# Attention of a four-layer encoder in pairs of heads: row-tiled scores, value matmuls of 512 columns, raw copies of q and k, an output projection with banks of its own

## The reference, cut to what matters

```python
for i in range(DEPTH):                      # DEPTH = 4, mixer i % 3
    h = rms_norm(x, attn_norm[i])
    proj = h @ w_in                         # 1024 x 3072 (FoX, REL) or 1024 x 1280 (SWA)
    q, k = rms_norm per head (16 heads of 64; SWA has 2 k/v heads, and rope)
    s = q @ k.T / 8 (+ cumulated log gates | + rel bias | window), masked
    o = softmax(s) @ v                      # SWA: one sink logit more in the softmax
    x = x + o @ w_o[i]
    x = x + conv_ffn(rms_norm(x, ffn_norm[i]), ...)
    x = x + sigmoid(rms_norm(x, ple_norm[i]) @ w_ple_gate[i]) * (p[i] @ w_ple_proj[i])
```

## Time and profile before

| | us |
|---|---|
| median of 3 runs (1481.05 to 1485.66) | 1484.01 |
| the profiled execution | 1480.81 |
| its span, first to last instruction | 1479.0 |
| PE busy | 1407.5 (95%) |
| DVE busy | 987.0 (67%) |
| ACT busy | 808.8 (55%) |
| POOL busy | 381.8 (26%) |

### The profile page before, as it was taken

The page is one execution under the profiler, slowest core; times in us unless marked ns, Lnnn a source line. Parts: engine busy times, 40 slices in busy tenths (PEclk is TensorE's granted clock), DMA queues, the critical chain, the costliest instruction groups (busy, mean ns, idle before and its releaser), DMA issues. The chain is left out here.

```text
span 1479.0 us, 24840 instructions
## 1 busy us (share of the span) xinstructions
PE 1407.5 (95%) x8532; PEld 1235.1 (84%) x8532; DVE 987.0 (67%) x1577; ACT 808.8 (55%) x1397; POOL 381.8 (26%) x437
## 2 busy tenths in 40 slices
PE   5999899999999999999987989999999999999998
PEld 4877799988777779998876779998878777999986
DVE  4657677764666867775476867776466575777644
ACT  4546566653555756664354656665356464666533
POOL 2311033320144603331027103332014110233200
PEclk9999999999999999999998899999999899999999
DMA  8522365564564345556552136666455322665651
GB/s 284 169 88 86 102 201 184 182 200 151 183 199 129 114 152 177 184 183 199 163 185 87 58 103 198 186 181 198 152 183 169 116 86 73 198 185 184 196 174 57
DMA packets 63959, 233.00 MB, mean 158 GB/s; under 512 B 7216, under 2 KB 7344, under 8 KB 63888
## 3 DMA queue, kind: packets, MB, share of 16 engines
q1 hardware_dynamic: 61056, 221.87, 46.7%
q0 software_dynamic: 2832, 10.18, 2.2%
HBM read 230.97 MB, written 1.05 MB: 157 GB/s over the span
## 5 line engine op out<-in xcount | busy, mean ns | idle before, releaser
L616 DVE TENSOR_TENSOR w_lo<-w_raw,w_hi 128x1024 fp32r<-128x1024 f32 x418 | 544.5, 1342 | 125.6 <-ACT w_hi L386 124.6
L386 ACT ACTIVATE w_hi<-w_raw 128x1024 fp32r<-128x1024 f32 x418 | 419.6, 1052 | 151.1 <-PE bank L1087 113.1
L1063 PE MATMUL bank<-hT_hi,w_hi 128*128 128x256 f32 x1408 | 398.7, 283 | 4.3 <-DVE hT_lo L670 4.3
L1064 PE MATMUL bank<-hT_lo,w_hi 128*128 128x256 f32 x1408 | 398.5, 283 | 0.0
L1065 PE MATMUL bank<-hT_hi,w_lo 128*128 128x256 f32 x1408 | 398.4, 283 | 0.0
L1063 PEld LDWEIGHTS bank<-hT_hi,w_hi 128*128 128x128 f32 x1408 | 270.3, 192 | 5.1 <-issue 5.1
L1064 PEld LDWEIGHTS bank<-hT_lo,w_hi 128*128 128x128 f32 x1408 | 270.3, 192 | 0.0
L1065 PEld LDWEIGHTS bank<-hT_hi,w_lo 128*128 128x128 f32 x1408 | 270.3, 192 | 0.0
L1049 POOL TENSOR_TENSOR gate_c<-gate_c,up_c 128x256 f32<-128x256 f32 x88 | 105.1, 1194 | 289.0 <-ACT gate_c L591 289.0
L901 DVE SCALAR_TENSOR_TENSOR gate_c<-bank,conv_sb,gate_c 128x255 f32<-128x255 f32 (+1 forms) x176 | 84.1, 478 | 116.2 <-ACT up_c L587 116.2
L1063 PE MATMUL bank<-w_hi,hT_hi 128*128 128x512 f32 (+1 forms) x336 | 137.3, 409 | 12.4 <-DVE w_lo L616 6.6
(11 more groups left out here) (141 smaller groups left out, 2237.1 us busy)
## 6 DMA issues: line engine op xcount, KB each, us to landing
w_raw<-weights SPq DMA_DIRECT2D x418, 512.0 KB, 4.0
gain<-gains POOLq DMA_DIRECT2D x11, 512.0 KB, 4.6
rel<-rel_in POOLq DMA_DIRECT2D x4, 512.0 KB, 6.5
x<-x_in SPq DMA_DIRECT2D x2, 512.0 KB, 6.5
p_raw<-p_in POOLq DMA_DIRECT2D x4, 256.0 KB, 5.0
out<-x SPq DMA_DIRECT2D x2, 512.0 KB, 2.6
gain<-gains SPq DMA_DIRECT2D x1, 512.0 KB, 7.0
consts<-consts_in POOLq DMA_DIRECT2D x1, 488.0 KB, 5.8
```

Of the source, the lines that this page charges most:

```text
L386: nc.scalar.activation(w_hi[:, slot, q * HALF:(q + 1) * HALF], w_raw[:, raw, :], ACT.Copy).then_inc(hi_ready, 1)
L616: nc.vector.tensor_tensor(w_lo[:, slot, cols], w_raw[:, half(q)[0], :], w_hi[:, slot, cols].bitcast(F32), ALU.subtract).then_inc(lo_ready, 1)
L1063: nc.tensor.matmul(out_ap, l_hi, r_hi, start=start, stop=False, skip_group_check=True)
L1064: nc.tensor.matmul(out_ap, l_hi, r_lo, start=False, stop=False, skip_group_check=True)
```

## The change

- **Order of the blocks**: q0, k0, q1, k1, v0, v1; the weights are laid out to match. The first eight pieces after the opening pair (blocks q1 and k1) come before the attention; the eight pieces of v0 and v1 come in steps 0 to 5 of it (2, 2, 1, 1, 1, 1).
- **Items**: ACT copies q or k raw into `qn` (now three deep) and squares it; PE may overwrite the bank after these two. POOL scales the item in `qn` (FoX, REL). In SWA DVE scales it and makes one rope product, POOL the other product and the sums.
- **Attention**: eight steps of a head pair. Scores alternate between the two row groups (rows 0 to 63 and 64 to 127) into two banks, and the first query tile sees only 128 keys. `sel` and `cum` are doubled to 64 rows in each group. All probabilities are scaled by POOL, none by DVE. The values of a pair are 3 matmuls of 512 columns (both heads) and 3 of 2x128 columns.
- **Banks**: transposed items in `aux[2..3]`; the output projection in `acc[0]`, `acc[1]`, `aux[0]`, `aux[1]`, so both token tiles of a unit can run together; embedding's projection in `aux[2..3]` and `acc[2..3]`, placed around the transposes of the norm.
- **Rest**: one `gain` buffer instead of two, the relative bias in pairs of heads and not negated, no zero blocks in `pT`.

```diff
+STEP_PIECES = {FOX: {0: (8, 9), 1: (10, 11), 2: (12,), 3: (13,), 4: (14,), 5: (15,)}, SWA: {}}
+ITEMS_AFTER_PIECE = {FOX: {1: (2,), 3: (3,), 6: (4,), 7: (5,)}, SWA: {0: (2,), 3: (3,)}}
+STEP_ITEMS = {FOX: {1: (6, 7)}, REL: {1: (6, 7)}, SWA: {1: (4,), 2: (5,)}}
+STEP_O = {FOX: {6: 0, 7: 1}, REL: {6: 0, 7: 1}, SWA: {5: 0, 7: 1}}
+STEP_V = {FOX: {2: (0, 1), 5: (2,), 6: (3,)}, SWA: {}}
+STEP_SPLITS = {FOX: {1: (16,), 2: (17, 18), 3: (19,), 4: (20,), 5: (21,), 6: (22,), 7: (23,)},
+               SWA: {0: (8,), 1: (9,)}}
 ...
 # ACT
+                for s in range(PAIRS + 3):
+                    if s >= 3:
+                        round_o(s - 3)
+                    if s < PAIRS:
+                        exps(2 * s)
+                        exps(2 * s + 1)
+                        if m == SWA:
+                            sink_exps(s)
+                    for i in STEP_ITEMS[m].get(s - 1, ()):
+                        copy_items(i)
+                    for j in STEP_V[m].get(s + 0, ()):
+                        evacuate_v(j)
+                    if 1 <= s <= PAIRS:
+                        round_pT(2 * s - 2)
+                        round_pT(2 * s - 1)
+                    for j in STEP_SPLITS[m].get(s, ()):
+                        split_half(first, j)
 ...
 # DVE
+                for s in range(PAIRS + 3):
+                    if s < PAIRS:
+                        mask_scores(2 * s)
+                        mask_scores(2 * s + 1)
+                        if m == SWA:
+                            sink_sums(s)
+                    if s >= 3:
+                        rest_o(s - 3)
+                    if m == SWA and s < 2:
+                        turn_item(4 + s)
+                    for i in STEP_ITEMS[m].get(s - 1, ()):
+                        rest_items(i)
+                    for j in STEP_V[m].get(s, ()):
+                        rest_v(j)
+                    if s < PAIRS:
+                        invert_sums(s)
+                    if 1 <= s <= PAIRS:
+                        rest_pT(2 * s - 2)
+                        rest_pT(2 * s - 1)
+                    for j in STEP_SPLITS[m].get(s, ()):
+                        split_half(first, j)
 ...
 # POOL: the items first, then the pairs
+                def normalise_p(h):
+                    for c, qb in ((slice(0, P), 0), (slice(P, 3 * P), 1)):
+                        nc.gpsimd.tensor_scalar(sc[:, h % SC, c], sc[:, h % SC, c], den[:, qb, h:h + 1], 1.0,
+                                                ALU.mult, ALU.mult).then_inc(pn_ready, 1)
+                for s in range(PAIRS):
+                    if m == REL and s + 2 < PAIRS:
+                        pool.wait_ge(s_min, 2 * (HEADS * L + 2 * s + 2))
+                        load_bias(s + 2)
+                    if m == REL and s and s + 1 < PAIRS:
+                        prepare_bias(s + 1)
+                    pool.wait_ge(rden_ready, PAIRS * L + s + 1)
+                    normalise_p(2 * s)
+                    normalise_p(2 * s + 1)
 ...
 # PE
+                def piece(j):
+                    i, g, t = todo[j]
 ...
+                        elif i == 4:
+                            pe.wait_ge(sq_ready, item0 + 4 + t + 1)
+                        else:
+                            pe.wait_ge(v_ready, FIRST_V[L] + t + 1)
 ...
+                def score_pair(pair):
 ...
+                    for qb in range(2):
+                        keys = P if qb == 0 else SEQ
 ...
+                        for left, right in ((qT_hi, kT_hi), (qT_hi, kT_lo), (qT_lo, kT_hi)):
+                            for e, r in enumerate(halves):
+                                last = nc.tensor.matmul(aux[e][:, cols], left[r, pair, ts], right[r, kp, 0:keys], ...
 ...
+                for s in range(PAIRS + 2):
+                    if s < PAIRS:
+                        score_pair(s)
+                    for j in STEP_PIECES[m].get(s, ()):
+                        piece(j)
+                    if s in STEP_O[m]:
+                        o_piece(STEP_O[m][s], 0)
+                    if s == PAIRS:
+                        o_piece(0, 1)
+                    if 1 <= s <= PAIRS:
+                        transpose_p(2 * s - 2)
+                        transpose_p(2 * s - 1)
+                    transpose_items(*STEP_ITEMS[m].get(s, ()))
+                    if s >= 2:
+                        values(s - 2)
+                    if s == PAIRS:
+                        o_piece(1, 1)
+                o_piece(2, 0)
+                o_piece(2, 1)
+                o_piece(3, 0).then_inc(tile_done, 1)
+                o_piece(3, 1)
```

More of the change, by code:

```diff
@@ L153, in trunk @@
         hT_lo = sb("hT_lo", [P, KC, SEQ], F32R)
-        gain = sb("gain", [P, 2, D])
+        gain = sb("gain", [P, D])
         ident = sb("ident", [P, P])
@@ L383, in split_hi @@
                     act.wait_ge(raw_landed[raw], loads * 16)
-                    if not first and q == 0:
+                    if not first and q == halves[0]:
                         act.wait_ge(unit_used, u - (RING - 1))
@@ L498, in evacuate @@
                         ins.then_inc(v_hi_ready, 1)
-                if L == 0:
[L501 to L525, removed]
@@ new lines, in _ @@
+                if m == SWA:
+                    item_rstd(0)
+                    turn_item(0)
+                    item_rstd(1)
+                    item_rstd(2)
+                    turn_item(1)
+                    turn_item(2)
+                    for i in range(3, len(ITEMS[m])):
+                        item_rstd(i)
+                        turn_item(i)
+                else:
+                    for i in range(len(ITEMS[m])):
+                        if i == 6 and m == REL:
+                            prepare_bias(0)
+                            prepare_bias(1)
+                        item_rstd(i)
+                        scale_item(i)
@@ L1230, in transpose_p @@
+                        if m == FOX:
+                            for e, r in enumerate(halves):
+                                h = 2 * pair + e
+                                last = nc.tensor.matmul(aux[e][:, cols], sel[r, h:h + 1].to_broadcast([HD, P]), cum[r, 0:keys],
+                                                        start=False, stop=True, skip_group_check=True)
+                                if qb == 1:
+                                    last.then_inc(s_done, 1)
                 def transpose_p(h):
@@ L1282, in _ @@
[L1282 to L1284 removed]
+                    if k == 0 and t == 0:
+                        if m == SWA:
+                            pe.wait_ge(sq_ready, item0 + 6)
+                        else:
+                            pe.wait_ge(v_ready, FIRST_V[L] + 4)
+                    if k == 0 and t == 1:
+                        pe.wait_ge(s_min, 2 * HEADS * (L + 1))
@@ L1342, in in_units @@
         out.append(w[:, :, -256:].transpose(1, 0, 2).reshape(P, UNIT))
-    for c in range(0, w.shape[2] - 511, 512):
+    for c in order or range(0, w.shape[2] - 511, 512):
         for g in range(2):
```

741 lines of the change are left out of this document (387 added, 354 removed).

## The result

The kernel after takes 1449.79 us, median of four runs (1449.07 to 1451.53), against 1484.05 for the kernel before (1481.05 to 1485.66): ratio 0.977, interval 0.9755 to 0.9791. It is faster, by 34 us. The prediction had 1420, so its sign and its range held, and 30 of the forecast 64 us did not come. The profiled execution went from a span of 1479.0 to 1447.0.

A forecast was written before the change was run, and what follows sets the result against it. PE's work and waits in the mixers were taken as the bound. Savings 2 x 17.8 + 8.3 + 3 x 3.1 + 6.5 + 3.6 = 63.3 us from 1480.8 gave 1417.5, 1420 for the runs; range 1397 to 1458.

The forecast's parts named there:

- Scores: PE's scores of a head pair: 1.1 us in FoX, 0.86 in REL or SWA, for 3.26 and 1.8 before.
- Rival 1: Scores: row groups don't overlap when each matmul brings its own weights; + 19 us, 1439; chance 8%.
- Values and transposes: PE work of a head pair: values 1.05 us for 2 x 0.72 before, transposes staying at 0.84.
- Pace of a step: Steps holding a pair and one piece: 5.75 us in FoX, taken as 5.7, and 5.5 in REL; PE sets it.
- Rival 2: Attention steps: DVE, ACT and POOL set the round, 6.5 us, as contention stretches them; + 23 us, 1443; chance 24%.
- The wait before piece 12: FoX and REL, step 2: PE waits 5.5 us for v0's copy before v1 overwrites its bank; slower clock 3 us.
- Rival 3: Step 2 of FoX and REL: the wait for v0 is short, as DVE is ahead; - 8 x 3, 1396; chance 11%.
- two output pieces to cover the last POOL work: End of FoX mixer: steps 8 and 9 with two output pieces, 8.5 us, within a mixer of 77.5.
- REL: REL mixer, first score to end of output projection: 75.6 us for 83.9, saved 8.3.
- Before the scores: FoX and REL: PE's waits for k items go and two items' transposes move behind; 3.1 us in each of three layers.
- Late next: nothing: FoX and REL, before the scores: no new wait follows; PE runs from piece 7 into step 0.
- SWA: SWA layer: 84 us for 90.5, saved 6.5, bounds -4 and 13; PE idle 11 us before first transposes of probabilities.

The follow-up runs named there:

- e3_rows_apart: Kernel after, with a pair's scores issued head by head, all of one row group and then the other: 1452.51 us, ratio 0.9801 to the kernel before.
- e5_dve_256: Kernel after, with scaling of the 256-column block of probabilities moved from POOL to DVE: 1452.49 us, ratio 0.9781 to the kernel before.
- e6_one_op: Kernel after, with POOL's scaling as one multiplication, without the second one by 1.0: 1453.26 us, ratio 0.9793 to the kernel before.
- e2_v_early: Kernel after, with block v0 copied out in step 1 (not 2) and v1 in steps 4 and 5 (not 5 and 6): 1412.26 us, ratio 0.9521.
- e1_v1_early: Kernel after, with block v1 alone copied out one step earlier, in steps 4 and 5 in place of 5 and 6: 1431.56 us, ratio 0.9642.
- e8_item5: e2_v_early, with item 5 of FoX and REL transposed in step 0 behind the first scores, not in front of them: 1408.09 us, ratio 0.9475.
- e4_swa_pool: Kernel after, with POOL in SWA scaling pairs 0 and 1 before it turns items 4 and 5: 1448.59 us, ratio 0.9756 to the kernel before.
- e7: e2_v_early, e8_item5 and e4_swa_pool together, against the kernel before: 1399.17 us, ratio 0.9431.

## Why the prediction was right or wrong

The mechanism held: PE set the pace of the FoX and REL steps, its work for a pair fell, and most of the gain came from the two FoX layers. One term was mis-sized, by an omitted wait.

*Scores.* Forecast 1.1 and 0.86, measured 1.10 and 0.88. Rival 1 is out: the row groups overlap, in e3_rows_apart even without the alternating order. The single place in the earlier trace rows was a fair witness.

*Values and transposes.* Forecast 1.05 and 0.84, measured 1.22 and 0.58, together 1.80 for 1.89: two errors that nearly cancel. Six transposes in one run cost less each than three (0.097 for 0.14), and the three 512-column matmuls behind them took 0.78 for 3 x 0.23. Both look like a price of each change of kind; that reading was not tested.

*Pace of a step.* Forecast 5.7 to 5.75 and 5.5, measured 5.78 and 5.57. Rival 2 is out for the kernel after, and in e5_dve_256 DVE has 0.87 us more in each step, and the step stays. But here the forecast had luck. It put POOL's scaling at 3.0 a pair, from the one-operand rows, and it takes 1.8, since the kernel writes it with two operands. In e6_one_op it takes 3.3, near the forecast's own price, and there rival 2's mechanism does reach PE, in one step of each FoX and REL mixer (6.7 us), 3 us in all and not its 23. By the rule of the Trainium skill that the prediction cited, SBUF — State Buffer, section Who interferes with whom, a DVE operation with two inputs in SBUF and a POOL operation that reads SBUF contend for a pair of ports under an exclusive lock. The trace agrees about the lock: a DVE addition of 4 columns takes 1.22 us beside POOL's 1.77 us product in SWA, where both end at 799.6, and 0.15 later. The same shows on the other side at 1182.8 in layer 3, where POOL's scaling of 128 columns takes 1.42 us beside a split, for 0.37 just ahead of it. It doesn't follow that each step loses by it; in the kernel after PE's step is 5.78 all the same:

```profile
797.84 1.77 POOL L1135 TENSOR_TENSOR rope_c<-qn,rtab 128x512 f32<-128x512 f32 x1 [0.81 <-DVE qn L814]
...
798.41 1.22 DVE L957 TENSOR_TENSOR den<-den,esink 128x4 f32<-128x4 f32 x1
...
810.03 0.15 DVE L957 TENSOR_TENSOR den<-den,esink 128x4 f32<-128x4 f32 x1
```

*The wait before piece 12.* Forecast 5.5 us and a lower clock behind it for 3 us; measured 5.6 and 5.8, then a piece of 4.6 to 5.1 us for 2.9, so 1.7 to 2.2 for the clock. Rival 3 is out as a forecast. As an experiment it came true: e2_v_early gained 19.3 over e1_v1_early; I had put its advantage at 24.

*The step that failed: the FoX and REL mixers' sum, in "two output pieces to cover the last POOL work".* I gave the output pieces of steps 6 to 9 no wait. But they use the banks of v as piece 12 does: the same semaphore, `v_ready`, at a count of 4 where piece 12 asks for 1. I had worked out who copies v0 and in which step, and had not asked the same of v1. In the kernel after it costs 5.9, 6.6 and 5.9 us of waiting and 1.6 to 2.0 at the lower clock behind each, 7.9 x 3 = 24 by these lengths. Taking it out gave 18.2 us in the median, and mixers of 77.5 and 75.8 us for the forecast 77.5 and 75.6. So in its mixers the kernel that I had predicted was e1_v1_early. That they agree to 0.2 us is partly luck: in layer 3 piece 12 cost 0.7 us less than charged there (5.6 + 2.2 for 8.5), and the step with the copy 0.6 more.

*REL*: forecast 8.3 saved, measured 0 (83.9 before and after); the missed wait (6.6 + 2.0) is all of it.

*Before the scores*: forecast 3.1 each, measured 1.8 in layer 0, 2.2 in REL and 0.8 in layer 3. "Late next: nothing" was wrong:

```profile
1129.33 0.66 PE L1276 MATMUL bank<-ident,qn 128*128 128x128 f32 x4 [0.33 <-POOL qn L1125]
...
1134.25 0.66 PE L1276 MATMUL bank<-ident,qn 128*128 128x128 f32 x4 [1.49 <-POOL qn L1125]
```

PE no longer waits for the k items, but for POOL's scaling of items 4 and 5, whose transposes stand in front of the scores. I had checked POOL's chain against item 7 only. e8_item5 took the wait out.

*SWA*: forecast 6.5 saved, measured 1.3 (89.2 for 90.5). PE's idle time was called at 11 us and was 10.6, but pair 0 was scaled from + 34.5 on, not at + 29.3: POOL's turns of items 3 to 5 took 3.4 to 4.5 us each and waited up to 4.5 for DVE's product. e4_swa_pool makes the layer 5.9 shorter.

*After the mixer*: forecast 0.9 a layer, measured 0.9 (10.3 to 9.3).

The bill, forecast less saved by layer: 6.8, 9.4, 6.9 and 8.1, together 31. The missed wait is 24 of them by its lengths, and 18 by the time or 21 by the mixers of e1_v1_early. SWA's start is 5, the waits before the scores another 4 to 5, and the way from layer 1's up projection to SWA's first items 2. The mixer of layer 0 had been 1.3 us shorter than layer 3's already before, which the forecast counted as gain. Against these stand about 2.5 for the shorter stretch behind piece 12, and the 2.7 by which layer 0 started sooner. It is the missed wait that made 1420 into 1450.

What stays open: why the granted clock falls behind a short wait in one kernel and not behind the same wait in another. In e4_swa_pool it took back 4 us of 5.9, and so it blurs what an edit of that size is worth. The length of the wait alone does not decide it. Before the first scores of layer 3 PE waits for 1.5 us in seven of the kernels; in the kernel after, e1, e2 and e6_one_op the clock stayed and the first step took 6.8 us, in e3, e4 and e5 it fell and the step took 8.3 to 8.4. The input projection of layer 3 starts behind two waits in every kernel, the second of 1.2 us in all. With a first wait of 1.1, 1.2, 1.3, 1.7 and 1.9 us (kernel after, e3, e5, before, e6_one_op) its 60 matmuls kept the full clock; with 1.4, 1.4, 1.4, 1.8 and 1.9 (e1, e8, e7, e2, e4_swa_pool) they lost it and took 15.2 to 16.6 us for 13.7. Two of the ten, e6_one_op and e1_v1_early:

```profile
1092.40:1106.10 13.70, 13.62 (x60) 11.29 (x61) 9.80 (x12) 8.23 (x12) 8.79 (x8) 1.00 0.60 191
1079.20:1094.50 15.30, 15.21 (x60) 12.45 (x61) 9.82 (x12) 8.24 (x12) 9.57 (x8) 0.89 0.52 167
```

No run here changed one short wait by itself.

## What to carry to other kernels

When a shared bank gets a new wait, list every later user of that bank with the semaphore count it needs and the step in which the copy is done, not only the first. A copy that frees a bank belongs in the step in which its matmuls end, not a step later behind that step's exponentials and masks: two edits of one table of step numbers were worth 37.5 us here, as much as the whole rebuild, although the step that took the copy became 0.5 to 1.0 us longer. And once a large wait is gone, look for the shorter ones that had stood in its shadow; a PE idle for 5.6 to 6.6 us paid 1.6 to 2.2 us more at the lower clock. A gain of a few us in one layer is read from that layer, with the granted clock of the next one beside it, before the run's time is believed.

## What the runs showed of the hardware

- Two row groups overlap when the program issues them one after the other, four matmuls apart: 1.18 us a pair against 1.10 alternating.
- With 64 rows, a pair of 128-column matmuls costs as much as a pair of 256 columns, 0.11 us each.
- POOL's multiplication by a value per partition took 1008 ns for 256 columns with one operand and 476 with two; for 128 columns 631 and 420 (means; beside a DVE split one of the 128-column ones took 1.42 us, and 0.37 ahead of it).
- After PE had been idle for 5.6 to 6.6 us, the next 12 matmuls took 4.5 to 5.1 us for 2.88 each time. After 1.5 us the clock was 1.00 in one kernel and 0.78, then 0.63 in another; after 1.9 and 1.2 us it was 1.00 in e6_one_op and 0.82 in e4_swa_pool, over the same 60 matmuls.
- A DVE addition of 4 columns took 1.22 us beside a POOL product, and 0.15 alone.
